# A gated DeltaNet scan: block inverses by one chain on 128 partitions, R in one fused operation, another order at the start

## The reference

```python
decay = where(incl, exp(gc[..., :, None] - gc[..., None, :]), 0)
m = where(strict, einsum('bhncd,bhnsd->bhncs', k * beta, k) * decay, 0)
a = m + eye                      # unit lower triangular
u = triangular_solve(a, v * beta)
w = triangular_solve(a, k * beta * exp(gc))
attn = where(incl, einsum('bhncd,bhnsd->bhncs', q, k) * decay, 0)
def step(s, inp):
    v_new = ui - wi @ s
    o = qd @ s + ai @ v_new
    s = s * exp(gl) + kd.T @ v_new
```

## Time and profile before

| | |
|---|---|
| median of 3 runs | 3703.55 us (3703.0 to 3704.4) |
| the profiled execution | 3708.23 us, span 3706.4 us |
| mean granted clock of TensorE | 0.966 |
| busy in the span: PE, DVE, ACT, POOL | 94%, 49%, 27%, 24% |
| the scan's first and last instructions | 644.5 us, about 1139 us |
| POOL's R operations (line 1535) | 36, 1.27 us each |
| DVE's chain operations (lines 1674 and 1675) | 252, median 0.32 and 0.33 us, up to 1.20 |
| POOL's chain operations (lines 1565 and 1566) | 252, median 0.28 and 0.29 us |

### The profile page before, as it was taken

How to read it: one execution, slowest core, us unless ns; L and a number is a source line. 1 busy time by engine, 2 the same in 40 slices (tenths; PEclk the granted TensorE clock), 3 DMA queues, 4 the chain that set the end, 5 groups by cost and what they waited for, 6 DMA issues and landing times. The chain is left out here.

```text
span 3706.4 us, 41570 instructions
## 1 busy us (share of the span) xinstructions
PE 3473.9 (94%) x15660; PEld 2202.6 (59%) x15660; DVE 1830.5 (49%) x2771; ACT 990.3 (27%) x1973; POOL 875.8 (24%) x874
## 2 busy tenths in 40 slices
PE   6999998789989998789999999999969999999998
PEld 2445443789985444444444444445558788788786
DVE  4454544677665553462222222234356666656666
ACT  4365556133334320221111111112201111111113
POOL 1022222565555400201011111123321212222211
PEclk9999999799999999999999999999959999999999
DMA  8222332556554413951111221134335656566566
GB/s 291 72 78 79 94 100 70 157 173 198 172 191 140 133 46 116 310 164 42 57 57 57 94 68 57 40 120 149 124 127 199 207 198 217 187 217 197 186 216 250
DMA packets 354831, 523.44 MB, mean 141 GB/s; under 512 B 50236, under 2 KB 225887, under 8 KB 354441
## 3 DMA queue, kind: packets, MB, share of 16 engines
q1 hardware_dynamic: 331316, 462.06, 37.2%
q0 software_dynamic: 12096, 43.84, 4.5%
q10 hardware_dynamic: 11221, 14.87, 1.1%
HBM read 410.85 MB, written 111.97 MB: 141 GB/s over the span
## 5 line engine op out<-in xcount | busy, mean ns | idle before, releaser
L2837 POOL TENSOR_TENSOR mg<-mg,sg_m 128x512 f32<-128x512 f32 x64 | 98.1, 1533 | 777.3 <-DVE sg_m L2718 777.3
L3724 PE MATMUL bank<-xeT,raw_e 128*128 128x128 f32 x2304 | 267.9, 275 | 0.8 <-ACT xeT L3568 0.8
L3724 PEld LDWEIGHTS bank<-xeT,raw_e 128*128 128x128 f32 x2304 | 263.6, 192 | 8.3 <-issue 8.3
L2624 PE MATMUL bank<-hT,raw_w 128*128 128x512 f32 x576 | 261.6, 597 | 5.2 <-PEq L2428 5.2
L957 POOL TENSOR_SCALAR sg<-tmp 128x512 f32<-128x512 f32 (+1 forms) x76 | 113.4, 1493 | 427.2 <-DVE tmp L1025 367.0
L2624 PEld LDWEIGHTS bank<-hT,raw_w 128*128 128x128 f32 x576 | 110.3, 192 | 144.2 <-issue 144.2
L3724 PE MATMUL bank<-T_e,U 128*128 128x128 f32 x1536 | 176.7, 275 | 0.0
L3724 PEld LDWEIGHTS bank<-T_e,U 128*128 128x128 f32 x1536 | 174.1, 192 | 0.0
L2624 PE MATMUL bank<-zT,S 128*128 128x512 f32 x384 | 172.6, 592 | 0.0
L685 PE MATMUL bank<-T_d,S_d 128*128 128x512 f32 x384 | 171.5, 593 | 0.0
L2718 DVE TENSOR_TENSOR sg_m<-sg_m,bank 128x512 f32<-128x512 f32 x64 | 43.9, 686 | 228.1 <-PE bank L2636 228.1
(11 more groups left out here) (540 smaller groups left out, 7145.2 us busy)
## 6 DMA issues: line engine op xcount, KB each, us to landing
raw_e<-in_exp_w_gate SPq DMA_DIRECT2D x16, 3072.0 KB, 16.5
raw_e<-in_exp_w_up SPq DMA_DIRECT2D x16, 3072.0 KB, 12.8
raw_e<-in_exp_w_down SPq DMA_DIRECT2D x16, 3072.0 KB, 10.3
raw_w<-in_w_in SPq DMA_DIRECT2D x24, 1024.0 KB, 5.7
raw_d<-in_w_in SPq DMA_DIRECT2D x16, 1024.0 KB, 5.9
raw_h<-in_w_in SPq DMA_DIRECT2D x12, 1024.0 KB, 5.3
x0T<-in_ada_w SPq DMA_DIRECT2D x44, 256.0 KB, 3.1
raw_h<-kT_d SPq DMA_DIRECT2D x36, 256.0 KB, 5.4
```

Of the source, the lines that this page charges most:

```text
L2624: mm = pe.matmul(bank[:, :], lhs[:, k, :], rhs[:, k, :], start=first and k == 0, stop=k == 3, skip_group_check=not first)
L2837: pool.tensor_tensor(mg[:, i, :], mg[:, i, :], sg[:, i, :], ALU.add).then_inc(add_ok[i], 1)
L3724: mm = pe.matmul(bank[:, f * P:(f + 1) * P], lhs[:, k, f * P:(f + 1) * P], rhs[:, k, :], start=fresh and k == 0, stop=k == 3, skip_group_c ...
```

## The change

The lower and the turned upper blocks are solved together. Partitions 0 to 63 of nb hold the blocks as before; the same blocks are loaded once more into partitions 64 to 127 of another place (raw_u) and copied, turned, into nb, so that the upper systems are lower ones too. One chain, `solve(eng, b, half)`, works on 128 partitions; its result for the upper blocks is turned back by one more copy. For block 0 it runs on DVE, for all others on POOL. DVE no longer has a chain in the steps. It has 32 operations (INV) where each of the two had 30.

R is formed by DVE alone: four `scalar_tensor_tensor` operations per direction, one for each head, product times negc plus vN, where negc is minus egc, made once. DVE now waits for vN; POOL's `difference_to_values` is gone.

Ahead of step 0, PE does the differences, then the key products, then the query products of fronts 0 and 1; the first merge level no longer waits for the attention of front 3; key_state and query_state of step 0 stand between the merge levels. POOL takes the masks of front 1 ahead of the gates of front 2, and waits for the whole of block 0's chain (on DVE) before the masks of front 3. DVE no longer waits for lv at its start. SP issues two more loads for each block.

```diff
+            def solve(eng, b, half):
+                x, t, n = nb[b % 2], Tb[:, b % 2, 0, :], [b * INV + (0 if half == 0 else 3 + 2 * (HALF - 1))]
...
+                if half == 0:
+                    if b >= 1:
+                        eng.wait_ge(inv, n[0])
+                    eng.wait_ge(nb_in[b % 2], 64 * (b // 2 + 1))
...
+                    link(eng.tensor_copy(t, unit))
+                    link(eng.tensor_copy(grid(x[64:128, :]), turned_grid(raw_u[b % 2])))
+                    link(eng.tensor_scalar(grid(t)[:, 1:ROWS, 0], x[:, 1:ROWS], -1.0, None, ALU.mult))
+                for k in (range(1, HALF) if half == 0 else range(HALF, ROWS - 1)):
+                    area = [P, ROWS - 1 - k, k + 1]
+                    work = prod[:, 0:(ROWS - 1 - k) * (k + 1)].rearrange("q (i c) -> q i c", c=k + 1)
+                    link(eng.tensor_tensor(work, x[:, k * ROWS + k + 1:(k + 1) * ROWS].unsqueeze(2).to_broadcast(area), grid(t)[:, k:k + 1, 0:k + 1].to_broadcast(area), ALU.mult))
+                    link(eng.tensor_tensor(grid(t)[:, k + 1:ROWS, 0:k + 1], grid(t)[:, k + 1:ROWS, 0:k + 1], work, ALU.subtract))
+                if half == 1:
+                    link(eng.tensor_copy(grid(Tb[64:128, b % 2, 1, :]), turned_grid(t[64:128, :])))
...
+                            sp.dma_start(raw_u[b % 2][32 * w:32 * w + 32, :].rearrange("q (i c) -> q i c", c=ROWS), padded(nc_d[f])[:, :, 0:ROWS]).then_inc(nb_in[b % 2], 16)
...
+                    pe.wait_ge(nc_ok, AHEAD - 1)
+                    merge_inner(0, 0)
+                    merge_outer(0, 0)
                     pe.wait_ge(at_ok, nth(AHEAD - 1, 1))
-                    for l in range(NL):
-                        merge_inner(0, l)
-                        merge_outer(0, l)
+                    merge_inner(0, 1)
+                    key_state(0, 0)
+                    merge_outer(0, 1)
+                    key_state(0, 1)
+                    merge_inner(0, 2)
+                    query_state(0, 0)
+                    merge_outer(0, 2)
+                    query_state(0, 1)
...
-                    upper_blocks(0, 0)
-                    upper_blocks(0, 1)
                     decays(3)
+                    pool.wait_ge(inv, INV)
                     for d in range(2):
                         masked(3, d)
...
-                        dve.tensor_tensor(R[:, d], b4(4 + 2 * d), per_token(egc, s, d), ALU.mult).then_inc(r1_ok, 1)
+                        dve.wait_ge(ldv[s % 2], 64 * (s // 2 + 1))
...
+                        for h in heads:
+                            last = dve.scalar_tensor_tensor(R[:, d, h, :], b4(4 + 2 * d)[:, h, :], column(negc, s, d, h), vN[:, s % 2, d, h, :], ALU.mult, ALU.add)
+                        last.then_inc(r_ok, 1)
...
-                        if s % 2 == 0 and s + 2 < STEPS:
-                            lower_blocks((s + 2) // 2, 1)
```

More of the change, by code:

```diff
@@ L1402, in output @@
                         mm4(4 + 2 * d, attn(s, d), V[:, d]).then_inc(out_mm, 1)
-                    for f in range(AHEAD):
+                    differences(0)
+                    differences(1)
+                    for f in range(2):
+                        for d in range(2):
+                            key_product(f, d)
+                    for f in range(2):
+                        for d in range(2):
+                            query_product(f, d)
+                    for f in range(2, AHEAD):
                         differences(f)
@@ L1539, in decayed_state @@
                         pool.tensor_tensor(S[:, d], S[:, d], per_token(etot, s, d), ALU.mult).then_inc(sx_ok, 1)
[L1541 to L1566, removed]
                     decays(0)
                     decays(1)
-                    for d in range(2):
-                        masked(0, d)
+                    for f in range(2):
+                        for d in range(2):
+                            masked(f, d)
                     decays(2)
                     for d in range(2):
-                        masked(1, d)
-                    for d in range(2):
                         masked(2, d)
-                    upper_blocks(0, 0)
-                    upper_blocks(0, 1)
                     decays(3)
+                    pool.wait_ge(inv, INV)
                     for d in range(2):
@@ L1651, in joined @@
                         dve.tensor_tensor(t, t, PS[2][:, :].rearrange("p (n t b) -> p n t b", t=2, b=b), ALU.subtract).then_inc(up_ok, 1)
[L1653 to L1668, removed]
-                            link(dve.tensor_copy(t, unit))
-                            link(dve.tensor_scalar(grid(t)[:, 1:ROWS, 0], x[:, 1:ROWS], -1.0, None, ALU.mult))
-                        for k in (range(1, HALF) if half == 0 else range(HALF, ROWS - 1)):
-                            area = [64, ROWS - 1 - k, k + 1]
-                            work = prod_f[:, 0:(ROWS - 1 - k) * (k + 1)].rearrange("q (i c) -> q i c", c=k + 1)
-                            link(dve.tensor_tensor(work, x[:, k * ROWS + k + 1:(k + 1) * ROWS].unsqueeze(2).to_broadcast(area), grid(t)[:, k:k + 1, 0:k + 1].to_broadcast(area), ALU.mult))
-                            link(dve.tensor_tensor(grid(t)[:, k + 1:ROWS, 0:k + 1], grid(t)[:, k + 1:ROWS, 0:k + 1], work, ALU.subtract))
                     def front(f):
@@ L1682, in front @@
                             attention(f, d)
-                    for f in range(AHEAD - 1):
-                        front(f)
-                    lower_blocks(0, 0)
-                    lower_blocks(0, 1)
+                    for f in range(2):
+                        for d in range(2):
+                            gram(f, d)
+                        gram_sum(f)
+                    for f in range(2):
+                        for d in range(2):
+                            attention(f, d)
+                    front(2)
+                    solve(dve, 0, 0)
+                    solve(dve, 0, 1)
                     front(AHEAD - 1)
```

65 lines of the change are left out of this document (35 added, 30 removed).

## The result

| | before | after |
|---|---|---|
| median | 3703.98 us (3703.0 to 3707.8) | 3646.15 us (3644.9 to 3649.8) |
| profiled execution, span | 3708.23, 3706.4 us | 3644.86, 3643.1 us |
| scan's first instruction to the next stage's first product | 498.67 us | 435.5 us |
| scan's first instruction to step 0's corrected product | 71.91 us | 61.53 us |
| K of step 1 to K of step 15 | 353.88 us | 305.28 us |

The ratio is 0.984, with a 95% interval of 0.983 to 0.985. The two profiled executions differ by 63.4 us and their scans by 63.2 us, so between these two the whole gain lies in the scan. The forecast was 63.8 for the scan and 3640 us for the median.

The account below looks back on a forecast made before the run. PE was taken to bound odd steps, waits for R and for E behind DVE's chain the even ones. Gains of 48.6 + 4.7 + 10.5 = 63.8 us off 3703.55 gave 3640 us, range 3634 to 3648.

Parts of the forecast that it names:

- The steady steps: Scan steps after the start: even steps fall to the odd steps' 22.08 us, step 14 to 18.25; gain 48.6 us.
- The width of a link: POOL's chain: a 128-partition link costs today's price, giving 5.7 us for the first half and 4.7 for the second.
- The slack: POOL's chain in even steps: it can end 1.6 us later than forecast before T comes too late.
- Step 0: From step 0's corrected product to K, the first product, of step 1: 20.5 us becomes 15.85, gain 4.7 us.
- The start: Ahead of step 0: first corrected product at 705.5 to 706 instead of 716.36; gain 10.5 us, bounds 7 and 13.
- the fronts 0 to 2 end up to 1.5 us earlier: Ahead of step 0: reordered products and masks let the chain begin at 668; bounds 0 and 2 us.
- the four state products in the gaps: Merges ahead of step 0: put into gaps of 0.78 us, they cost 0 to 1 us each, 1.5 in all.
- rival 2: Start goes otherwise: merges at 2.4 GHz give 3636 us, or chain and front 3 no earlier gives 3650; chance 0.12.
- the difference of 4.7 us is taken as constant: Whole kernel: profiled execution's 3708.23 us minus the sister runs' median 3703.55 was assumed to stay the same.
- (1) T late: Even steps: POOL's chain ends 3 us past its slack, each keeps about 3 us; gain 40, 3664 us; chance 0.16.
- (3) Double link price: POOL's chain: width counts and links cost double, pair 53.9 us, total 3711 us, deciding from about 0.6 per link; chance 0.05.
- (4) Other waits in the even steps: PE's even steps refill with other waits, for instance loads coming closer together; near 3703 us; chance 0.03.

Follow-up runs that it names:

- slack_half1: Changed kernel with each product of the second half of POOL's chain computed twice (7 more links, not for block 0): 3653.99 us, ratio 0.986.
- run 2: Kernel before with only R formed in the fused DVE operations, both chains and the start's order as before: 3684.09 us, ratio 0.994.
- run 4: Changed kernel with the order of before ahead of step 0 (PE, POOL and DVE): 3656.78 us, ratio 0.987.
- run 9: Changed kernel with another order ahead of step 0, DVE running block 0's chain before front 2: 3641.58 us, ratio 0.983.
- Early_chain: The same as run 9: changed kernel with block 0's chain ahead of front 2 on DVE, 3641.58 us.
- runs 1 and 10: Changed kernel unedited, measured a second and a third time: 3649.1 us (ratio 0.984) and 3647.86 us (ratio 0.985).
- run 1: Changed kernel unedited, measured a second time: 3649.1 us, ratio 0.984.
- slack_both: Changed kernel with each product in both halves of POOL's chain computed twice (14 more links, not for block 0): 3671.57 us, ratio 0.992.
- old_start: The same as run 4: changed kernel with the order of before ahead of step 0, 3656.78 us.
- slack_double: Changed kernel with each product of POOL's chain computed three times (28 more links, not for block 0): 3706.23 us, ratio 1.001.
- Fused_r_only: The same as run 2: kernel before with only R fused on DVE, 3684.09 us.
- chain_on_dve: Changed kernel with its one 128-partition chain run by DVE instead of POOL in the steps: 3706.92 us, ratio 1.002.
- runs 2 and 5: First run 2; second chain_on_dve, the changed kernel with its one chain on DVE in the steps, 3706.92 us.

## Why the prediction was right, and where it was off

**The steady steps: right, for the stated reasons.** Both parities at 22.08, step 14 at 18.24: 48.60 us less from K of step 1 to K of step 15, where 48.6 were forecast. The times within step 8 came within 0.7 us: R at K + 3.3 (3.5 forecast), first half to 5.9 (5.5), first mask 9.2 (8.8), second half 15.9 (15.2), T 2.7 us after K (2.9). A turned copy takes 0.62 us (0.5), the pair draws 208 GB/s (206).

**The width of a link.** Taking today's price was the riskiest choice of the sum. It held: POOL's 128x63 product takes 0.29 us where the 64x63 one took 0.29. The slope over elements per partition had told it.

**The slack** was put at 1.6 us. In steps 2 and 12 the chain passed it by 1.2 us (second half to K + 18.0 where K + 16.8 was allowed), and nobody waited. I had counted the trip of the blocks through memory at its 8.2 us of step 6; from the store to T's first use it took 6.8 to 8.5 us in after and 6.5 to 7.6 in slack_half1. There 7 more links (2.5 us) are hidden in five of the eight odd steps, but not in three: of the 2.5 us, 1.6 reach T on average, and PE waits where T comes 4.8 us or more after K.

**Step 0**: 721.37 − 705.53 = 15.84 us, as forecast (15.85).

**The start: the sum right, two terms wrong.** The forecast was a corrected product at 705.5 to 706, and it came at 705.53. But "the fronts 0 to 2 end up to 1.5 us earlier" failed: the chain began at 671.2 and not at 668, because PE's query products of front 1 wait for DVE in the new order. T was 3.4 us late. And the four state products in the gaps did not cost 1.5 us; the merges were 2.0 us shorter than before's 18.9 with them inside, 3.5 off the sum, because the clock rose. That the state products lift it is likely and not shown alone. In the three traces without them in the gaps (before, runs 2 and 4) it is low from the first level's second product to the last join. Of the eight traces with them, run 9 aside, it rises during the first one in five, but in the other three it rose before it, and why is open. Early_chain shows the end of this (12.9 us at 1.00). The rule of the Trainium skill, "TensorE: Matmul & The Clock Gate", Part 1, is that steady work releases 2.4 GHz; these traces agree with it so far that the clock was low after PE's idle time (9.10 us in after) and at the full level where PE had more to do. This is rival 2's mechanism, though its time didn't come, since the late chain took the gain. That the total was right here is luck: a late chain and faster merges cancelled, and the same order gave 59.5 to 63.4 us in other traces.

**The step that failed: "the difference of 4.7 us is taken as constant".** The scan gave 63.2 of the forecast 63.8, the profiled executions 63.4, the medians only 57.8. Before's profiled execution lay 4.7 us above the median of 3703.55 that the sum starts from, after's 1.3 us below its own. Those 6.0 us, and 0.4 that the profiled executions gained less than forecast, are the 6.4 between 3639.75 (3703.55 − 63.8) and 3646.15. The executions of one kernel on one chip spread over 2 to 15 us. In runs 1 and 10 of the changed kernel this comes from the stage outside the scan. It isn't what set before's profiled execution apart: from the end of the scan to the first product with yaT and bw it took 529.97 us, after's 530.28, the two shortest of all the traces, and run 1's 537.8.

So before's offset most likely lies in its scan, though no second trace of it shows this. Outside the scan the twelve traces take 3207.6 to 3216.4 us, and before's, with 3207.7, is at the lower end. Other executions of before took as little as 3697.8 us. Unless they were faster outside the scan than any trace here, their scans were some 10 us shorter than the 498.67 of the trace. By this estimate the profiled execution of before had a long scan, a typical scan gain is nearer the medians' 55 to 58 us than 63.2, and so the exact match of the scan with the forecast (63.2 against 63.8) is in part luck.

**The rivals.** (1) T late: no. The chain would have to pass its slack by some 3 us; slack_both, with 5 us more of chain, comes near it (3671.57 us where the rival had 3664). (2) The start otherwise: its clock part came, see above; its other part (the chain no faster and front 3 no earlier) is nearly old_start, 8.6 us of scan against the 10.5 priced. (3) Double link price: not so, and slack_double shows what it would have cost: first half to K + 10.6 (11 forecast), second to K + 25.6 (25.6), T to K + 32.5 (33.8), PE waits of 2.22 and 1.51 us where 3.9 and 3.3 were priced, total 3706 us where 3711 were. The turning point is near 0.7 us per link, not 0.6. (4) Other waits in the even steps: none, PE is busy throughout the pair.

**What the prediction did not see** is why before's even steps were long. It counted DVE's second half at 9 us as work removed. Fused_r_only and chain_on_dve show that half of that (9.0 against 4.4 us) was DVE's links standing beside POOL's long operations. The forecast was right without this, since the change takes the chain off DVE altogether.

## What to carry to other kernels

Put a chain of small dependent operations on the engine whose small operations keep their price beside the other's long ones, here GpSimd, even if each is somewhat slower alone (0.30 against 0.22 us). Where a stretch is a ladder of PE product, DVE, ACT and back, fill the gaps with independent products: it pays in the work moved, and here most likely in the clock too. And make the sum for the stage that changes, by its own first and last rows, but from more than one trace where that stage has waits; an offset between one profiled execution and a median is no constant, and here it was nearly the whole error.

## What the runs showed of the hardware that was not expected

- A DVE operation on two SBUF tiles of 55 to 63 elements takes 0.22 us alone and 0.89 to 1.23 beside POOL's 128x512 operations, which keep their 1.02 or 1.25 us each (runs 2 and 5 and before). Beside POOL's own small links it takes 0.32 to 0.36 (run 2). A DVE operation with one operand in PSUM kept its time (2.16 us for both directions of R). The chain at the start took 13.2 us beside them and 8.1 without (run 4). The Trainium skill, "SBUF — State Buffer", section "Who interferes with whom", tells of an exclusive lock between the two engines; the trace agrees, and the numbers here are its price for small operations. POOL suffers too: one copy took 1.13 us instead of 0.62 where DVE's sum of two Gram matrices ran beside it.
- A small POOL operation costs the same on 64 and on 128 partitions (0.29 us for 63 elements).
- The granted clock of nearly the same merges was 0.50, 0.69, 0.87 and 1.00 (run 4, after, slack_both, run 9); their time was 19.6, 16.9, 14.2 and 12.9 us. After and slack_both have the same order there, so the order alone doesn't fix the clock.
